# Expert weights of the last ten pairs loaded as whole matrices, one 2-MiB transfer each, instead of two 1-MiB halves

## What is computed

```
for e in range(N_EXPERTS):                                  # 32
    hid = jax.nn.silu(t @ w_eg[e]) * (t @ w_eu[e])          # (1024, 512) each
    out = out + gates[:, e:e + 1] * (hid @ w_ed[e])         # (512, 1024)
```

## Time and profile before

| | |
|---|---|
| time, median of 3 runs | 1785.64 us (1783.07, 1785.64, 1787.6) |
| span of the profiled execution | 1782.6 us (no device time of its own is listed) |
| TensorE busy | 1755.3 us, 98% |
| TensorE clock granted, mean | 0.997 |
| expert stage on TensorE | from 167.4 us (first matmul on `mring`) to 615 us (last) |
| weight transfers of the stage | 192 of 1024 KB: 190 into `mring`, 2 into spare buffers |

### The profile page before, as it was taken

The page is one execution under the profiler, slowest core; times in us unless marked ns, Lnnn a source line. Parts: engine busy times, 40 slices in busy tenths (PEclk is TensorE's granted clock), DMA queues, the critical chain, the costliest instruction groups (busy, mean ns, idle before and its releaser), DMA issues.

```text
span 1782.6 us, 24689 instructions
## 1 busy us (share of the span) xinstructions
PE 1755.3 (98%) x9808; PEld 1335.7 (75%) x9808; DVE 954.3 (54%) x1254; ACT 727.6 (41%) x1008; POOL 41.1 (2%) x55
## 2 busy tenths in 40 slices
PE   9999999999999999999999999999999999999998
PEld 8886444544445488888988888878888879888886
DVE  6584111111111286666787666676666864666665
ACT  5562111111111254345566434664346445553445
POOL 2000000000000000000000000000000001200000
PEclk9999999999999999999999999999999999999999
DMA  9277999999999955554435555365555544555551
GB/s 307 96 259 302 404 421 418 419 422 422 422 422 422 359 204 187 187 186 148 142 119 186 188 188 189 129 225 189 188 189 192 189 154 154 185 188 189 188 189 60
DMA packets 191209, 428.80 MB, mean 241 GB/s; under 512 B 7292, under 2 KB 145632, under 8 KB 166560
## 3 DMA queue, kind: packets, MB, share of 16 engines
q1 hardware_dynamic: 187952, 418.41, 64.4%
q0 software_dynamic: 3184, 9.36, 1.6%
HBM read 426.69 MB, written 1.05 MB: 240 GB/s over the span
## 4 chain that ended last, share of the span: by engine, by line
PE 89%; DVE 7%; ACT 3%; issue 1%; DVEq 0%; ACTq 0%
PE pw L534 64%; PE acc L534 23%; DVE wl L1928 1%; PE pw L916 1%; ACT arena L1692 1%; DVE x L2377 0%; ACT sm L1523 0%; DVE sm L2635 0%; DVE scr L2466 0%; DVE scr L2632 0%; ACT wh L1362 0%; PE pw L949 0%; PE pw L1290 0%; ACT arena L1670 0%; DVE scr L2648 0%
## 5 line engine op out<-in xcount | busy, mean ns | idle before, releaser
L534 PE MATMUL pw<-aa,wh 128*128 128x512 f32 (+1 forms) x2288 | 670.1, 357 | 2.3 <-DVE aa L1946 1.3
L534 PE MATMUL pw<-aa,wl 128*128 128x256 f32 x1880 | 528.0, 281 | 0.0
L1928 DVE TENSOR_TENSOR wl<-raw,wh 128x2048 fp32r<-128x2048 f32 x204 | 460.9, 2297 | 98.0 <-ACT wh L1362 95.5
L534 PEld LDWEIGHTS pw<-aa,wh 128*128 128x128 f32 x2288 | 404.7, 190 | 74.2 <-issue 3.4
L1362 ACT ACTIVATE wh<-raw 128x2048 fp32r<-128x2048 f32 x204 | 380.1, 1907 | 51.4 <-DMA raw<-in_odd_w_in 25.0
L534 PEld LDWEIGHTS pw<-aa,wl 128*128 128x128 f32 x1880 | 356.7, 190 | 1.6
L534 PE MATMUL acc<-wh,aa 128*128 128x512 f32 x1088 | 347.8, 393 | 2.2 <-DVE aa L2471 1.8
L534 PE MATMUL pw<-mring,arena 128*64 128x512 f32 x1520 | 333.6, 594 | 0.0
L534 PEld LDWEIGHTS pw<-mring,arena 128*64 128x64 f32 x1520 | 106.5, 137 | 201.0 <-issue 198.8
L534 PEld LDWEIGHTS acc<-wh,aa 128*128 128x128 f32 x1088 | 204.2, 188 | 48.9 <-DVE aa L2471 3.5
L534 PE MATMUL acc<-wl,aa 128*128 128x512 f32 x544 | 212.0, 390 | 0.0
(11 more groups left out here) (429 smaller groups left out, 1272.3 us busy)
## 6 DMA issues: line engine op xcount, KB each, us to landing
raw<-in_ffn_w_in SPq DMA_DIRECT2D x88, 1024.0 KB, 5.1
mring<-in_w_ed SPq DMA_DIRECT2D x64, 1024.0 KB, 16.7
mring<-in_w_eg SPq DMA_DIRECT2D x63, 1024.0 KB, 12.6
mring<-in_w_eu SPq DMA_DIRECT2D x63, 1024.0 KB, 14.5
raw<-in_ffn_w_out SPq DMA_DIRECT2D x44, 1024.0 KB, 5.0
raw<-in_odd_w_in SPq DMA_DIRECT2D x24, 1024.0 KB, 5.2
raw<-in_w_in SPq DMA_DIRECT2D x12, 1024.0 KB, 9.9
raw<-in_even_w_in SPq DMA_DIRECT2D x11, 1024.0 KB, 5.3
```

Source lines behind the costliest of these rows:

```text
L534: return pe.matmul(out, lhs, rhs, start=start, stop=stop, skip_group_check=True)
L1928: dve.tensor_tensor(wl[:, u % RING, :], raw[:, u % RING, :], wh[:, u % RING, :].bitcast(F32), ALU.subtract).then_inc(sig(f"{ep}_lo"), 1)
```

## The change

Pairs 6 to 15 are loaded by whole matrices. `whole` issues one DMA of 16 KB a partition into two neighbouring slots, so `M_SLOT` is renumbered (units n and n + 2 are now neighbours) and the second place of the down units gets a table, `E_SLOT`. A whole matrix n waits for the use of unit n + 2, where the first half waited for the use of unit n. The DMA raises the landing semaphore of n; the one of n + 2 is raised by SyncE at issue, since TensorE has already waited for n when it comes to n + 2. The down matrices of the very last pair stay in halves. The loads of pairs 0 to 5 stay units of 1 MiB, in a slightly different order at the start.

```diff
--- before.py
+++ after.py
@@ -248,7 +248,8 @@
         NA = 16
         PAIRS = E // 2
         PU = 2 * RING
-        M_SLOT = [4, 5, 10, 11, 0, 6, 1, 7, 2, 8, 3, 9]
+        M_SLOT = [4, 10, 5, 11, 0, 6, 1, 7, 2, 8, 3, 9]
+        E_SLOT = {8: 12, 10: 13, 9: 14, 11: 15}
         UB, n = {}, 0
         for l in range(2):
             for name, count in (("ffn1", 33), ("mix_in", 11 if l == 0 else 24), ("mix_out", 4 if l == 0 else 8),
@@ -345,20 +346,20 @@
                     sp.wait_ge(sig("heads_ready"), 5)
                     expert_unit(0, 0, "held", "e_landed")
             last_on = {(NA - 1 - d) % RING: NA - 1 - d for d in range(RING)}
-            for n, first in ((0, 2), (2, 0), (1, 2), (3, 0)):
+            for n, first in ((0, 2), (1, 2), (2, 0), (3, 0)):
                 sp.wait_ge(sig("a_used"), RING + last_on[M_SLOT[n] % RING] + 1)
                 expert_unit(n, first)
             sp.wait_ge(sig("a_used"), RING + 12)
-            for n in (8, 9):
-                expert_unit(n, of_pair(n), 2 * RING + n - 8, "e_landed")
+            for n in (8, 10):
+                expert_unit(n, of_pair(n), E_SLOT[n], "e_landed")
             sp.wait_ge(sig("heads_normed"), 2)
             expert_unit(1, 0, "held", "e_landed")
             for n in range(4, 8):
                 sp.wait_ge(sig("a_used"), RING + last_on[M_SLOT[n] % RING] + 1)
                 expert_unit(n, of_pair(n))
             sp.wait_ge(sig("a_used"), RING + NA)
-            for n in (10, 11):
-                expert_unit(n, of_pair(n), 2 * RING + n - 8, "e_landed")
+            for n in (9, 11):
+                expert_unit(n, of_pair(n), E_SLOT[n], "e_landed")
             for n in range(8, PU):
                 expert_unit(n, 2 + of_pair(n))
             for n in range(2, 8):
@@ -372,7 +373,7 @@
                     if odd:
                         expert_unit(n, expert + of_pair(n))
                     else:
-                        expert_unit(n, expert + of_pair(n), 2 * RING + n - 8, "e_landed")
+                        expert_unit(n, expert + of_pair(n), E_SLOT[n], "e_landed")
 
             def gate_up_units(expert, used):
 
@@ -385,10 +386,35 @@
                 for odd in range(2):
                     down_units(q * 4 + (4 + 2 * odd), odd, q * (2 * PU) + odd * PU)
                     gate_up_units(q * 4 + (4 + 2 * odd), q * (2 * PU) + (odd + 1) * PU)
-            with sp.Fori(0, PAIRS // 2 - 3) as q:
+            def whole(n, expert, slot, used, landed="m_landed"):
+
+                sp.wait_ge(sig("m_used"), used + (n + 3))
+                sp.wait_ge(sig("x_loaded"), 16)
+                wt = (a["w_eg"], a["w_eu"])[n % 2] if n < 8 else a["w_ed"]
+                k = KC if n < 8 else 4
+                src = wt[0, bass.ds(expert + of_pair(n), 1)].rearrange("o (p k) n -> p (o k n)", k=k)
+                dst = mring[:, slot:slot + 2, :].rearrange("p s n -> p (s n)")
+                sp.dma_start(dst, src).then_inc(sig(f"{landed}{n}"), 16)
+                sp.sem_inc(sig(f"{landed}{n + 2}"), 16)
+
+            def gate_up_whole(expert, used):
+
+                for n in (0, 1, 4, 5):
+                    whole(n, expert, M_SLOT[n], used)
+
+            def down_whole(expert, odd, used):
+
+                for n in (8, 9):
+                    whole(n, expert, M_SLOT[n] if odd else E_SLOT[n], used, "m_landed" if odd else "e_landed")
+
+            def two_pairs(q, last):
                 for odd in range(2):
-                    gate_up_units(q * 4 + (12 + 2 * odd), q * (2 * PU) + (odd + 5) * PU)
-                    down_units(q * 4 + (12 + 2 * odd), odd, q * (2 * PU) + (odd + 4) * PU)
+                    gate_up_whole(q * 4 + (12 + 2 * odd), q * (2 * PU) + (odd + 5) * PU)
+                    (down_units if last and odd else down_whole)(q * 4 + (12 + 2 * odd), odd, q * (2 * PU) + (odd + 4) * PU)
+
+            with sp.Fori(0, PAIRS // 2 - 4) as q:
+                two_pairs(q, False)
+            two_pairs(PAIRS // 2 - 4, True)
             sp.wait_ge(sig("rounds_ready"), 1)
             nr = sp.value_load(nrounds_i[0:1, 0:1], min_val=0, max_val=ROUNDS - 1)
             with sp.If(nr > 0):
@@ -926,7 +952,7 @@
                         for half in range(2):
                             for e in range(2):
                                 n = 8 + 2 * j + e
-                                slot = M_SLOT[n] if odd else 2 * RING + n - 8
+                                slot = M_SLOT[n] if odd else E_SLOT[n]
                                 wt = mring[:, slot, cc * D + half * 512:cc * D + (half + 1) * 512]
                                 last = mm(pw[CAP * e:CAP * (e + 1), 1 - half, :], hid[:, e, c, :], wt, c == 0, c == 3)
                                 if cc == 1 and half == 1:
```

## The result

The changed kernel takes 1789.81 us in the median of 8 runs (1787.92 to 1790.04), the kernel before 1785.21 us in the median of its 8 (1783.07 to 1787.6). The ratio is 1.0021 with a 95% interval of 1.0012 to 1.003: slower by 2 to 5 us. The prediction had 1787.3 us, in a range of 1784.0 to 1792.5. One run of the kernel before, among those taken beside the later experiments, took 2179.93 us at a granted clock of 0.752 and is left out of all medians and ratios.

A forecast was written before the change was run, and what follows sets the result against it. TensorE was taken to set the end while the slower DMA lives on its lead; a 1.9 us wait for whole matrices less 0.2 us gives +1.7 us on the median 1785.64, so 1787.3 us, range 1784.0 to 1792.5.

The forecast's parts named there:

- TensorE sets the pace, DMA lives on a lead, more DMA speed gives only 0.2 us: Expert stage: TensorE takes 28.25 us a pair, DMA 29.90; the lead lasts almost to the end, only 0.24 us is waited.
- Cost 1: Last pair: both whole matrices must land before expert 0 starts, at 589.6 against a want at 586.6, 3.0 us late.
- Gain, a turn of 4.90 us: Queue turn of a whole matrix: 4.90 us instead of 4.984 for two units, through 9 packets fewer, 0.08 us.
- The sum: Pair 15's second matrix lands at 588.5, a 1.9 us wait from 586.6, less 0.2 at expert 1: +1.7 us.
- Cost 2: Pair 6: whole matrices are issued later, so the queue is empty for 2.6 us; the third's turn starts at 323.9 earliest.
- Where it would show: TensorE's period stays 28.25 us up to pair 13, then `gate_up(0)` stretches in pairs 14 and 15, 1.9 us in all.
- Periods that stretch much earlier than pair 14: Stated sign of being wrong in the expert stage: turn underestimated, or the queue empty in other places.
- the forecast's own case: Whole-matrix turn of 4.87 to 4.94 us, costing +0 to +4 us; chance 0.50.
- the second rival: A small gain: a packet costs about a third as much, turn 4.955 us, +4.7 us, 1790.3 us; chance 0.12.
- No gain from the larger transfer: Rows cut to 8 KB, or 9 ns only for short rows: turn 4.984 us, +6.3, 1791.9 us; chance 0.17.
- A turn under 4.86: Whole matrices turn in 4.86 us or less, nobody waits: -0.2, 1785.4 us; chance 0.18.
- Faster by over 5.4 us: TensorE would have to wait that long for DMA before the change in the timed runs; chance 0.03.

The follow-up runs named there:

- the version with 8-KB rows: The changed kernel with the two halves of a matrix in slots that aren't neighbours, still one 2-MiB transfer; ratio 1.0051 to the kernel before.
- the last version: Kernel before with down matrices whole in pairs 6 to 15 (last one in halves), gate and up whole in pairs 10 to 13 alone; ratio 1.0001.
- fewer loads: Kernel before without the second halves of the down matrices in pairs 6 to 15 (20 of 120 units); 1784.37 us, ratio 0.9991.
- gate and up alone: The changed kernel with only gate and up matrices whole, all down matrices in halves; ratio 1.0024 to the kernel before.
- halves late: The changed kernel with all transfers in halves, gate and up units of pairs 6 to 15 issued as late and ordered as whole matrices; ratio 1.002.
- down first: The changed kernel with both down matrices of pair 6 ahead of its gate and up matrices; single run, trace only, last block +3.3 us.

## Why the prediction was right, and where it was off

- *TensorE sets the pace, DMA lives on a lead, more DMA speed gives only 0.2 us.* Right for the traced execution: 607.95 against 608.14 with a sixth of the loads gone. For the runs it stays open, whose median fell by 1.3 us there.
- *Cost 1, 3.0 us.* Right: +2.9 us in the trace when it stands alone.
- *Gain, a turn of 4.90 us.* Right: 4.892, and for the reason given, the price of a row. The sum counted the saved completion like a row, 9 packets of 9 ns; the version with 8-KB rows gives 8 rows of 10 ns and next to nothing for the completion.
- *Cost 2, the queue empty for 2.6 us, and 0.3 us at the third matrix.* This is the term that was mis-sized. The third matrix landed at 331.7 instead of 328.8. I had taken "2.5 us fixed, then its turn" from a unit into an idle queue. The whole matrix into the idle queue took 7.8 us, 2.9 beside its turn and not 2.5. The third came while the queue was running out: behind the second at 324.1 its turn would have ended at 329.0, and it landed 2.7 us later. The filler in pair 6 (the version with a down matrix between) takes that away. The empty time itself was as forecast, 2.6 us.
- *Where it would show.* A wait in `gate_up(0)` alone: right. From pair 14 on: wrong, it began in pair 11, because 2.9 us more were missing and the lead shrinks by 29.37 - 28.25 = 1.1 us a pair. Periods that stretch much earlier than pair 14 were a sign of being wrong by the prediction's own words, and it was met.
- *The sum.* Predicted 588.5 for the landing that decides, 591.0 measured; +1.7 us predicted, +4.4 in the stage. The ratio of the runs says +2 to +5 us. It was inside the range, at the upper edge of the forecast's own case (+0 to +4 us). That room was meant for the turn, which came out as forecast, and the entry filled it: that part is luck. The time is near the second rival's number, but not for that rival's reason: the turn was as forecast.
- *Rivals.* No gain from the larger transfer: false, and its price, +6.3 us, was borne out by the version with 8-KB rows (+7.8 us, with 2.1 us of the entry in it and 0.6 less for the turn). A small gain, a turn of 4.955: false. A turn under 4.86: false. Faster by over 5.4 us: false.
- *A slip in the expectations.* The versions with whole down matrices have 18 of them, not 19; the lead that the last version wins is 34 x 0.08 = 2.7 us.

Why the rows are slow after the queue has run low, I can't settle. What the traces show is the loss beyond the turn and the empty time, by the work left in the queue at the issue:

| load | work left, us | lost, us |
|---|---|---|
| first of expert 0: fewer loads, pairs 7 to 15 | 0 to 1.2 | 0 to 0.1 |
| first of expert 0: six versions with late or whole loads | 0 to 1.0 | 0.1 to 0.7 |
| first of expert 0: halves in pair 6, whole from pair 8 | 3.0 to 3.4 | 0 |
| first of expert 1: fewer loads, pairs 7 to 15 | 2.2 to 2.6 | 0.5 to 2.0 |
| first of expert 1: the change, gate and up alone, halves late, down first | 2.2 to 2.6 | 1.5 to 2.7 |
| first of expert 1: halves in pair 6, whole from pair 8, whole with 8-KB rows | 3.0 to 3.2 | 0 to 2.6 |
| all with more work left, in pairs 6 to 8 | 3.9 and more | 0 to 0.5 |

It happens with 8-KB rows and with halves too. An empty queue costs little beside its empty time. All losses over 0.7 us fall on the first load of expert 1 with 3.2 us of work left or less, and the first load of expert 0 lost nothing at 3.0 us. So a short queue alone may not be the whole cause; what else belongs to this place in the pair was not tested.

## What to carry to other kernels

Where a queue of loads is the slower resource and lives on a lead, count in the lead: a larger transfer lands later for its first user, and is issued later if it needs more space free, and both costs fall due in the last round, not where they arise. A transfer whose space has long been free (here the down matrices) can be enlarged at no cost. And look at the moments at which the queue nearly runs out: there a transfer can cost more than its turn plus the idle time (up to 2.7 us here).

## What the runs showed that I had not expected

- A load queue with 2.6 us of work left when a 2-MiB transfer was issued gave 309 GB/s at a DMA share of 0.92 for 6 us; with 7 us of work left it gave 437 GB/s in the same stretch. The loss goes with the place in the pair as well (the table above).
- Half as many completion packets saved 0.01 us a matrix at most (4.972 us against two units); half as many rows saved 0.080 us.
- Executions of the same kernel differ by 4 us, and the difference goes with the granted clock. Of the 87 runs of the kernel before in the experiments' series, the 30 with a mean clock of 0.998 took 1784.5 us on average, the 39 with 0.997 1785.7, the 14 with 0.996 1787.0 and the 4 below 1789.1. The traces show the steps. The version with fewer loads is 0.2 us ahead of the kernel before at 616 us and 1.35 us behind it at 620: from 616 to 626 us its clock is 0.83 and the other's 1.00. Near 1170 us it is the other way round (1.00 against 0.85), and the 1.5 us come back. So one such stretch is worth about 1.5 us, a third of the whole effect measured here; what decides which executions have it, the runs don't show. The windows from 616 to 626 us, fewer loads first, then the kernel before:

```profile
616.00:626.00 10.00, 8.71 (x31) 7.12 (x32) 6.71 (x14) 7.97 (x18) 0.00 (x0) 0.83 0.75 252
```

```profile
616.00:626.00 10.00, 8.51 (x37) 6.87 (x37) 7.44 (x15) 8.35 (x20) 0.22 (x1) 1.00 0.74 241
```
